# Barrier blocks joined at two seams of a kernel with a hybrid mixer and latent attention

## The reference, cut to what matters

```python
merged = (gates[:, :, 0] * (y_gla @ proj_gla) + gates[:, :, 1] * (y_ml @ proj_ml)
          + gates[:, :, 2] * (y_s5 @ proj_s5))
y = merged @ w_out                                    # the output linear
x = x + (1.0 + gt1) * rms_norm(y, post1_w[l])
h = rms_norm(x, pre2_w[l]) * (1.0 + sc2) + sh2        # then the SwiGLU layer
...
q = (rms_norm_2(c_q, mla_q_norm[j]) @ mla_w_uq[j])    # 12 heads of 64 + 32 (rotated)
kv = (rms_norm_2(c_kv, mla_kv_norm[j]) @ mla_w_ukv[j])
tok = causal_attention(q, k, v)
mem_out = memory_attention(q_mem, mem_k, mem_v)
y = jnp.concatenate([tok, mem_out], axis=-1) * jax.nn.silu(gate)
```

## Time and profile before

| | before |
|---|---|
| median of 3 runs | 3154.27 us (3153.13 to 3154.8) |
| the profiled execution | 3151.59 us |
| its span in the profile | 3149.8 us |
| mean granted TensorE clock | 0.953 of full |
| PE busy | 2916.0 us, 93% of the span |
| weight load (PEld) busy | 2211.8 us, 70% |
| DVE, ACT, POOL busy | 1516.7, 1073.2, 1001.0 us |

### The profile page before, as it was taken

How to read it: one execution, slowest core, us unless ns; L and a number is a source line. 1 busy time by engine, 2 the same in 40 slices (tenths; PEclk the granted TensorE clock), 3 DMA queues, 4 the chain that set the end, 5 groups by cost and what they waited for, 6 DMA issues and landing times. The chain is left out here.

```text
span 3149.8 us, 34726 instructions
## 1 busy us (share of the span) xinstructions
PE 2916.0 (93%) x14282; PEld 2211.8 (70%) x14282; DVE 1516.7 (48%) x1613; ACT 1073.2 (34%) x1455; POOL 1001.0 (32%) x527
## 2 busy tenths in 40 slices
PE   6999999999997989799999899999799998999887
PEld 5777777777775567577888687777566666777555
DVE  4263012325336361655555336342357674748567
ACT  3342222212216122423333345334334432337313
POOL 3232111113532121445545345342133331333102
PEclk8989999999998999899999999999889999999899
DMA  7111114662113342212222435322300002121201
GB/s 291 46 54 54 54 63 138 198 205 79 61 61 128 121 173 87 80 59 89 81 81 81 159 115 194 109 68 78 130 24 21 15 21 74 60 87 34 97 14 54
DMA packets 86175, 286.54 MB, mean 91 GB/s; under 512 B 8849, under 2 KB 13217, under 8 KB 84865
## 3 DMA queue, kind: packets, MB, share of 16 engines
q1 hardware_dynamic: 86018, 284.33, 26.9%
HBM read 219.70 MB, written 64.59 MB: 90 GB/s over the span
## 5 line engine op out<-in xcount | busy, mean ns | idle before, releaser
L280 POOL TENSOR_TENSOR w_lo_sb<-raw_w_sb,w_hi_sb 128x1024 fp32r<-128x1024 f32 x195 | 483.8, 2482 | 1388.6 <-ACT w_hi_sb L271 1388.5
L288 PE MATMUL ps<-h_hi_sb,w_hi_sb 128*128 128x512 f32 x720 | 300.8, 418 | 10.0 <-PEq L535 5.4
L288 PE MATMUL ps<-h_lo_sb,w_hi_sb 128*128 128x512 f32 x720 | 289.0, 401 | 0.0
L271 ACT ACTIVATE w_hi_sb<-raw_w_sb 128x1024 fp32r<-128x1024 f32 x195 | 205.3, 1053 | 219.4 <-PE ps L288 161.3
L288 PE MATMUL ps<-h_hi_sb,w_lo_sb 128*128 128x512 f32 x720 | 251.3, 402 | 0.0
L288 PE MATMUL ps<-merged_parts_hi_sb,w_hi_sb 128*128 128x512 f32 x472 | 191.2, 405 | 18.2 <-PEq L535 7.3
L288 PE MATMUL ps<-z_lo,w_hi_sb 128*128 128x512 f32 x512 | 204.6, 400 | 0.0
L288 PE MATMUL ps<-merged_parts_lo_sb,w_hi_sb 128*128 128x512 f32 x472 | 188.1, 399 | 0.0
L288 PE MATMUL ps<-merged_parts_hi_sb,w_lo_sb 128*128 128x512 f32 x472 | 179.3, 402 | 0.0
L288 PEld LDWEIGHTS ps<-h_hi_sb,w_hi_sb 128*128 128x128 f32 x720 | 138.2, 192 | 55.1 <-issue 22.5
L288 PE MATMUL ps<-z_hi,w_hi_sb 128*128 128x512 f32 x384 | 162.0, 422 | 14.2 <-PEq L910 5.6
(11 more groups left out here) (647 smaller groups left out, 6565.7 us busy)
## 6 DMA issues: line engine op xcount, KB each, us to landing
raw_w_sb<-in_w SPq DMA_DIRECT2D x231, 512.0 KB, 3.6
ada_late_sb<-in_ada SPq DMA_DIRECT2D x32, 512.0 KB, 3.6
inbox_sb<-gates_out SPq DMA_DIRECT2D x24, 512.0 KB, 4.1
ffn_hidden_out<-ffn_hidden_box_sb SPq DMA_DIRECT2D x22, 512.0 KB, 6.2
ffn_hidden_sb<-ffn_hidden_out SPq DMA_DIRECT2D x22, 512.0 KB, 4.7
ada_w<-in_ada SPq DMA_DIRECT2D x16, 512.0 KB, 8.7
gates_out<-outbox_sb SPq DMA_DIRECT2D x16, 512.0 KB, 2.6
inbox_sb<-sums_out SPq DMA_DIRECT2D x16, 512.0 KB, 5.1
```

The source lines that it names most:

```text
L271: nc.scalar.activation(w_hi[:, n % RING].rearrange("p t m -> p (t m)"), raw_w[:, n % RAW], ACT.Copy).then_inc(w_rounded.sem, 1)
L280: nc.gpsimd.tensor_tensor(w_lo[:, n % RING].rearrange("p t m -> p (t m)"), raw_w[:, n % RAW], flat_hi, ALU.subtract).then_inc(w_split.sem, 1)
L288: mm = nc.tensor.matmul(o, wt, xs, start=start and part == 0 and xs is x_hi, stop=stop and part == 1, skip_group_check=again)
```

## The change

The third merging and the output linear are one block now: the parts of the merging go into the `side_by_side` of the output linear, which starts at `merged.end`, and each of its first uses of an input tile waits for that tile's `merged_parts_lo`. The merging leaves no slot to the next block (`keep` 0). The load of x, which lies over memory that the merging uses, waits until the first tile of the output linear has been taken. The two waiting blocks, `begin` and the block of constants are gone as blocks: their steps are the first of SP, POOL, ACT and DVE in the attention's own block, each behind the waits for the output boxes and the memory heads; PE has none of these waits, and the maxima and ACT's copy of the values wait for the constants.

```diff
-                         None if split_to else (outbox, lambda m: sums_out[n][:, m]), jobs, needs, keep=1)
+                         None if split_to else (outbox, lambda m: sums_out[n][:, m]), jobs, needs, keep=keep)
...
+                part.split_s = lo_s
...
-            side_by_side(parts_of_y(), merge_part(0.0, 2, 1, YP, scope, None, PAIRS, 1.0, MP, None, parts_there))
+            y_parts = parts_of_y()
+            merged = merge_part(0.0, 2, 1, YP, scope, None, PAIRS, 1.0, MP, None, parts_there, 0)
...
-            mixed = dense(0.0, 8, 8, moving(MP), ["act"] * 8, emit, PAIRS, jobs=LATE_HALVES)
+
+            def merged_there(k, h):
+                return [merged.split_s.at(k + 1)] if h == 0 else []
+            mixed = dense(merged.end, 8, 8, moving(MP), ["act"] * 8, emit, PAIRS, jobs=LATE_HALVES, needs=merged_there)
...
             def begin_x0(sp):
-                yield -1.0
+                yield mixed.job_end[(0, (0, 1))] + 2.0
+                sp.wait_ge(act_free.sem, mixed.freed[0])
                 sp.dma_start(x0[:], a["x"]).then_inc(x0_s.sem, 16)
...
-            side_by_side(*parts, hidden, Part(begin_x0))
+            side_by_side(y_parts, merged, *parts, hidden, Part(begin_x0))
...
+                            opening.loads(sp)
...
+                            opening.emptied(pool)
...
+                                if causal and u == 0 and b == 0:
+                                    pe.wait_ge(*opening.done.at(1))
...
+                        if causal:
+                            opening.emptied(act)
...
+                            if part == "V" and u == 0:
+                                act.wait_ge(*opening.done.at(1))
...
+                        if causal:
+                            opening.constants(dve)
...
-                outbox.emptied()
-                finish(mem_z_s)
+                emptied = [(count.sem, count.n) for count in outbox.sems] + [(mem_z_s.sem, mem_z_s.n)]
...
-            begin([(g_s, g[:], closing_out), (g_s, Z[:, 6:8], mem_z_out)])
...
-            with nc.Block() as block:
-                @block.vector
-                def _(dve):
+            constants_s = sem_again("attention_constants")
+
+            class Opening:
+
+                done = constants_s
+
+                def loads(self, sp):
+                    self.emptied(sp)
+                    sp.dma_start(g[:], closing_out).then_inc(g_s.sem, 16)
+                    sp.dma_start(Z[:, 6:8], mem_z_out).then_inc(g_s.sem, 16)
+                    g_s.n += 32
+
+                def emptied(self, eng):
+                    for wait in emptied:
+                        eng.wait_ge(*wait)
+
+                def constants(self, dve):
+                    self.emptied(dve)
+                    for b in range(2):
+                        nc.vector.tensor_copy(kr[64:QK + 1, b], kh[64:QK + 1, 0]).then_inc(keys_s.sem, 1)
                     for j, name in enumerate(("ident", "mask_qk", "mask_kq")):
                         nc.vector.tensor_copy(masks_r[:, j], C(name))
-                    nc.vector.memset(vh[:], 1.0)
-                    for b in range(2):
-                        nc.vector.tensor_copy(kr[64:QK + 1, b], kh[64:QK + 1, 0]).then_inc(keys_s.sem, 1)
                     dve.wait_ge(*keys_s.at(2))
                     for b in range(2):
                         nc.vector.tensor_tensor(low[1][64:96, b], kh[64:96, b], kr[64:96, b].bitcast(F32),
                                                 ALU.subtract)
-            over([(keys_s, 2)])
+                    nc.vector.memset(vh[:], 1.0).then_inc(constants_s.sem, 1)
```

More of the change, by code:

```diff
@@ L1355, in gate_to_memory, with merge_part @@
             return part
-        def merge_part(at, n, b, parts, scope, outbox, banks, pace=1.0, split_to=None, jobs=None, needs=None):
+        def merge_part(at, n, b, parts, scope, outbox, banks, pace=1.0, split_to=None, jobs=None, needs=None, keep=1):
             inbox = sb_in(scope, f"inbox{n}", [P, 1 + (n > 0), 2, T])
@@ L2624, in build @@
         with ExitStack() as scope:
-            hi_s, lo_dve, lo_pool = sem_again("ml_hi"), sem_again("ml_lo_dve"), sem_again("ml_lo_pool")
+            y_hi_s, y_lo_dve, y_lo_pool = sem_again("ml_hi"), sem_again("ml_lo_dve"), sem_again("ml_lo_pool")
             def parts_of_y():
@@ L2630, in on_act @@
                         yield -8.0 + 1.1 * t
-                        nc.scalar.activation(YP[0][:, t], Y[:, t], ACT.Copy).then_inc(hi_s.sem, 1)
+                        nc.scalar.activation(YP[0][:, t], Y[:, t], ACT.Copy).then_inc(y_hi_s.sem, 1)
                 def rest(eng, vec_eng, first, count):
@@ L2635, in rest @@
                         yield -6.8 + 1.1 * t
-                        eng.wait_ge(*hi_s.at(t + 1))
+                        eng.wait_ge(*y_hi_s.at(t + 1))
                         vec_eng.tensor_tensor(YP[1][:, t], Y[:, t], YP[0][:, t].bitcast(F32), ALU.subtract
                                               ).then_inc(count.sem, 1)
-                return Part(None, None, on_act, lambda dve, link: rest(dve, nc.vector, 0, lo_dve),
-                            lambda pool, link: rest(pool, nc.gpsimd, 1, lo_pool))
+                return Part(None, None, on_act, lambda dve, link: rest(dve, nc.vector, 0, y_lo_dve),
+                            lambda pool, link: rest(pool, nc.gpsimd, 1, y_lo_pool))
             def parts_there(k, h):
-                return [hi_s.at(k + 1), (lo_dve, lo_pool)[k % 2].at(k // 2 + 1)]
-            side_by_side(parts_of_y(), merge_part(0.0, 2, 1, YP, scope, None, PAIRS, 1.0, MP, None, parts_there))
-            over([(hi_s, 4), (lo_dve, 2), (lo_pool, 2)])
+                return [y_hi_s.at(k + 1), (y_lo_dve, y_lo_pool)[k % 2].at(k // 2 + 1)]
+            y_parts = parts_of_y()
+            merged = merge_part(0.0, 2, 1, YP, scope, None, PAIRS, 1.0, MP, None, parts_there, 0)
         y_scope.close()
@@ L2818, in begin_x0 @@
                 sp.wait_ge(stored.sem, stored.n)
-            side_by_side(*parts, hidden, Part(begin_x0))
+            side_by_side(y_parts, merged, *parts, hidden, Part(begin_x0))
+            over([(y_hi_s, 4), (y_lo_dve, 2), (y_lo_pool, 2)])
             over([(x0_s, 16), (sq_s, 12), (acc_s, 11), (app_s, 16), (res_s, 16), (sq2_s, 16), (acc2_s, 14),
@@ L3335, in heads_in_halves, with attention @@
             return emit
-        def attention(iters, U, dq, keys_n, scale, q_of, k_of, v_of, out_of, sfx, rounded, project=None, gating=None):
+        def attention(iters, U, dq, keys_n, scale, q_of, k_of, v_of, out_of, sfx, rounded, project=None, gating=None,
+                      opening=None):
             causal = project is not None
@@ L4417, in build @@
                       lambda i, u: Z[64 * (u % 2):64 * (u % 2) + 64, u // 2],
-                      "_t", lambda u: (qr[:, u % 2], kr[:, u % 2]), project=project, gating=Gating())
+                      "_t", lambda u: (qr[:, u % 2], kr[:, u % 2]), project=project, gating=Gating(),
+                      opening=Opening())
+            over([(constants_s, 1), (keys_s, 2)])
         lru_scope = ctx.enter_context(ExitStack())
```

## The result

| | us |
|---|---|
| changed kernel, median of 4 runs | 3131.97 (3129.15 to 3141.67) |
| kernel before, median of 4 runs beside them | 3153.7 (3152.11 to 3154.8) |
| ratio, 95% interval | 0.9932 [0.9918, 0.9946] |
| profiled execution, its span | 3131.24, 3129.5 |

A forecast was written before the change was run, and what follows sets the result against it. PE, busy 93% of the span, was taken as the bound, with time to win from idling and half clock at two seams: 8.9 + 6.7 = 15.6 us off 3154.27 gives 3138.7 us, range 3133 to 3146.

The forecast's parts named there:

- The first seam: Between the merging's last matmul and the output linear's first: joining gains 6.3 us idle and 2.6 us half clock, 8.9 us.
- The cover over the eighth tile: At the output linear's start: merged tile 7 is ready 4 us before PE wants it, 1.8 us with POOL's interference.
- The second seam: At the token attention's opening, up to the first head's transposes: they start 6.7 us earlier, bounds 6.3 and 8.6.
- POOL's hold: In the rotation of the first head's queries: POOL's L4369 blocks DVE's addition of two SBUF tiles, costing 1.9 us.
- POOL does not hold DVE: Rival at the attention's opening: the rotation runs undisturbed beside POOL, 8.9 + 8.6 = 17.5 us gained, 3136.8; chance 0.18.
- the clock takes part back: Rival: longer PE idle before the transposes slows the second head's projection by 4.6 us; 11.0 us gained, 3143.3; chance 0.15.
- one seam pays nothing: Rival: a missed wait takes the barrier's place at either joined place; 3145.4 or 3147.6 us; chance 0.08.
- weights starve with the load of x: Rival in the output linear: weight loads queue behind x's 4 MB; at T = 75, 9.5 us slower, 3163.8; chance 0.02.
- All behind each seam moves up unchanged: Step for the rest of the program: later stretches keep their length, so the whole 15.6 us reaches the total.
- less 1 for the spread of the runs: Term in the range's low end, 3133: 1 us off for how much the runs vary.
- one more or less slow stretch: Term in the range's low end: 2.6 us off 3136.8, the half-clock price between merging and output linear.
- Theory B: From the experiments: the change gives 21 to 22 us, by a way that the sum did not have.

The follow-up runs named there:

- the second measurement: The change once more, unaltered, beside the kernel before on one chip: 3138.4 us (3134.04 to 3140.56), ratio 0.9945; the kernel before had a median of 3153.96 us.

## Why the prediction was right and wrong

**The first seam was right.** 8.9 us were forecast as 6.3 of idle time and 2.6 of half clock, and 8.91 came. PE never stopped, so the clock stayed at 1.00. The cover over the eighth tile was 2.6 us, where the text had 4 without POOL and 1.8 with it. The step held by POOL was the addition L1370 (2.44 us for 1.23), which reads two SBUF tiles, and not the rest of the tile, L1390. The load of x was issued 13.8 us after the merging's end (some 14 forecast); moving it on costs nothing. Awaiting the whole tail without the barrier lost the entire gain again.

**The second seam was right to 0.4 us.** From the issue of the heads' DMA to the transposes 17.55 us were forecast (2283.1 - 2265.55), and 17.11 came (2269.21 - 2252.10). PE started 1.14 us after the issue, 0.85 forecast; the constants took 6.42 us, 6.33 forecast; the bound moved to DVE as said, and the two kernels that shorten DVE's row behind the landing, by POOL's hold or by the memset as well, moved the transposes by 1.4 and 3.6 us. The term that was too large is POOL's hold: 1.3 us for one L3725, where 1.9 had been taken. POOL's L4399 began 12.0 us behind PE's restart instead of 11.45, so the first addition was through and only the second was held. Where POOL began 0.3 us ahead of the first addition, in the kernel with only the second seam, that addition took 2.57 us, a hold of 1.9.

**The rivals.** That POOL does not hold DVE fell with 1.98 us against 0.68, and with the kernel that starts POOL later. That the clock takes part back fell too: PE idled 6.07 us ahead of the transposes instead of 2.2, yet the 34 matmuls behind took 12.89 us instead of 12.82, and all behind them 832.99 instead of 832.82, where 4.6 us more had been reckoned with. The Trainium skill (TensorE: Matmul & The Clock Gate, What's actually happening) says that the slow clock is the default and activity releases it; the trace agrees at the first seam (1.00 without idle time, 0.60 behind 7.1 us of it in the kernel that waits), and at the second the longer idle time had nothing more to take, since the clock was at its lower level there already: 0.50 in the 10 us behind the transposes, as before. Behind the first seam, though, the clock did take 1.4 to 1.6 us back and returned 0.5 to 1.4 of it later, a term that neither the sum nor this rival had. That one seam pays nothing fell with the two kernels that have one seam each, and that weights starve with the load of x moved on.

**The step that failed** is the one that turns a gain in the seams into a time: "All behind each seam moves up unchanged", together with "less 1 for the spread of the runs" and "one more or less slow stretch" at the low end. The sum was right for the two seams, 15.6 us for 16.0, and the untouched stretches were taken as fixed. They are not: in the first profile they were shorter by 3.24 + 1.31 - 0.17 - 0.07 = 4.3 us. That measurement had three of four runs at 3129.15 to 3132.7 us; the 17 runs of the same kernel in the three later measurements lie between 3134.04 and 3144.89, with medians of 3138.4, 3139.16 and 3138.99, 15.6, 14.0 and 16.5 us under the kernel before (forecast 3138.7 and 15.6). Theory B is thereby gone for these. That two of the three gains lie within 1 us of 15.6 is partly luck, since a median of so few executions strays by that much. The three runs of before that I had seen lay within 1.7 us and suggested a spread of 1 us; the 25 of the second measurement lie between 3148.07 and 3162.04. The stretch near 200 us differs by the clock granted to identical instructions: its 200 matmuls took 31.40 us at a clock of 0.78, 30.6 at 0.83 and 27.5 at 0.94. What decides it within an execution, and why the first four runs fell so well together, stays open: the four measurements were made at different times, the later three on three chips, and no run here separates these.

## What to carry to other kernels

A barrier costs what it uncovers: price the tail behind it that other work could hide and the half clock after the idle time, not its own instructions, and look at which engine's row of small steps then ends last. Once such a row bounds a seam, move what nobody needs yet behind the step that is awaited, on the same engine; handing it to GpSimd can hold VectorE for as long as it saves. Judge a change of a few us by the distance between the same two matmuls around it, over several profiles, and let the range of a forecast of the total hold the stretches that the change does not touch.

## What the hardware showed that was not expected

- Thirteen profiles of the same first 1.18 ms of program span 9.2 us (1175.33 to 1184.50), and the same 200 matmuls in it took 31.40, 30.63 or 27.50 us at a granted clock of 0.78, 0.83 or 0.94.
- A GpSimd memset of 1.80 us that reads nothing held the first of two VectorE casts of 33x1024: 2.97 us for both instead of 1.29. A VectorE addition of 32x512 took 1.90 to 2.57 us beside a GpSimd subtraction, 0.68 without; in each of the eight profiles where it was held it ended 0.55 us behind the subtraction.
- VectorE's memset took 1.76 us for 2048 columns and 0.48 for 512.
- All eleven profiles without the barrier at the first seam lose 1.4 to 1.6 us of clock in the same 100 matmuls, some 100 us behind it.
